# A three-way split GEMM decoder layer: the third weight tile's matmuls moved into the opening phase, five clears moved to GpSimd, and two orders changed further on

## What is computed

```python
h = rms_norm(x, norm1)
z = h @ w_in                        # 2048 x 5120: u (1024), q, f, i, g (1024 each)
pool_out = pool_mix(u)              # means over windows 2/4/8/16, a small map per group
o, S_new = hgrn2_recurrence(silu(q), 1 - forget, i, log(forget), S)   # 8 heads, state 128 x 128
o = rms(o) * hg_norm * silu(g)
x = x + concat(pool_out, o) @ w_o   # 2048 x 2048
h2 = rms_norm(x, norm2)
x = x + (silu(h2 @ w_gate) * (h2 @ w_up)) @ w_down                    # 2048 x 5632, twice, and back
return rms_norm(x, norm_f), pool state, recurrent state
```

## Time and profile before

| | |
|---|---|
| median of 3 executions | 1398.15 us (1397.76 to 1398.55) |
| the profiled execution | 1397.94 us |
| its span | 1396.1 us |
| PE busy | 1380.8 us, 10128 matmuls |
| VectorE, ScalarE, GpSimd busy | 787.9, 571.9, 204.8 us |
| mean granted clock of PE | 0.997 |

### The profile page before, as it was taken

The page is one execution under the profiler, slowest core; times in us unless marked ns, Lnnn a source line. Parts: engine busy times, 40 slices in busy tenths (PEclk is TensorE's granted clock), DMA queues, the critical chain, the costliest instruction groups (busy, mean ns, idle before and its releaser), DMA issues.

```text
span 1396.1 us, 27712 instructions
## 1 busy us (share of the span) xinstructions
PE 1380.8 (99%) x10128; PEld 1368.7 (98%) x10128; DVE 787.9 (56%) x1202; ACT 571.9 (41%) x924; POOL 204.8 (15%) x320
## 2 busy tenths in 40 slices
PE   9999999999999999999999999999999999999996
PEld 8999999999999999999999999999999999999996
DVE  7978888888655544444444444444444444444444
ACT  7546665566333333333333333333333333333442
POOL 0464444444322000000000000000000000000131
PEclk9999999999999999999999999999999999999998
DMA  9446555555655555555655545565554565555453
GB/s 321 149 124 172 163 152 152 152 157 163 176 148 150 141 157 140 150 138 145 165 147 151 150 132 146 154 169 150 150 150 121 155 172 149 152 143 149 113 157 119
DMA packets 395563, 214.50 MB, mean 154 GB/s; under 512 B 4287, under 2 KB 391487, under 8 KB 394886
## 3 DMA queue, kind: packets, MB, share of 16 engines
q1 hardware_dynamic: 377063, 203.52, 52.5%
q10 hardware_dynamic: 18470, 10.59, 2.6%
HBM read 206.43 MB, written 7.89 MB: 154 GB/s over the span
## 4 chain that ended last, share of the span: by engine, by line
PE 96%; DVE 2%; issue 1%; ACT 1%; DMA 0%; SPq 0%; DVEq 0%; ACTq 0%
PE bank L405 30%; PE bank L407 30%; PE bank L406 30%; DVE w_lo L1086 1%; DMA x_res<-in_x_turned 0%; PE bank L607 0%; DVE yg L1532 0%; PE bank L653 0%; PE bank L582 0%; PE bank L655 0%; PE bank L654 0%; PE bank L445 0%; PE bank L447 0%; PE bank L446 0%; PE bank L536 0%
## 5 line engine op out<-in xcount | busy, mean ns | idle before, releaser
L405 PE MATMUL bank<-a_hi,w_hi 128*128 128x320 f32 x2016 | 626.3, 311 | 0.1
L407 PE MATMUL bank<-a_hi,w_lo 128*128 128x320 f32 x2016 | 623.8, 309 | 0.0
L406 PE MATMUL bank<-a_lo,w_hi 128*128 128x320 f32 x2016 | 623.7, 309 | 0.0
L1086 DVE TENSOR_TENSOR w_lo<-w_raw,w_hi 128x1024 fp32r<-128x1024 f32 (+1 forms) x412 | 456.5, 1148 | 134.3 <-ACT w_hi L743 133.0
L743 ACT ACTIVATE w_hi<-w_raw 128x1024 fp32r<-128x1024 f32 (+1 forms) x412 | 383.3, 967 | 159.6 <-PE bank L407 144.8
L405 PEld LDWEIGHTS bank<-a_hi,w_hi 128*128 128x128 f32 x2016 | 378.6, 188 | 2.6 <-issue 2.1
L406 PEld LDWEIGHTS bank<-a_lo,w_hi 128*128 128x128 f32 x2016 | 378.7, 188 | 0.4
L407 PEld LDWEIGHTS bank<-a_hi,w_lo 128*128 128x128 f32 x2016 | 378.6, 188 | 0.0
L405 PE MATMUL bank<-h_hi,w_hi 128*128 128x320 f32 x704 | 217.7, 309 | 0.3 <-DVE w_lo L1086 0.3
L406 PE MATMUL bank<-h_lo,w_hi 128*128 128x320 f32 x704 | 217.6, 309 | 0.0
L407 PE MATMUL bank<-h_hi,w_lo 128*128 128x320 f32 x704 | 217.6, 309 | 0.0
(11 more groups left out here) (247 smaller groups left out, 1152.2 us busy)
## 6 DMA issues: line engine op xcount, KB each, us to landing
w_raw<-in_w_gate SPq DMA_DIRECT2D x44, 1024.0 KB, 5.6
w_raw<-in_w_up SPq DMA_DIRECT2D x44, 1024.0 KB, 5.6
w_raw<-in_w_down SPq DMA_DIRECT2D x64, 704.0 KB, 4.8
w_raw<-in_w_in SPq DMA_DIRECT2D x32, 1024.0 KB, 5.8
w_raw<-in_w_o SPq DMA_DIRECT2D x16, 1024.0 KB, 6.0
w_raw<-in_w_first_pool SPq DMA_DIRECT2D x5, 1024.0 KB, 5.5
s<-in_state_hgrn ACTq DMA_DIRECT2D x8, 512.0 KB, 4.4
out<-sn ACTq DMA_DIRECT2D x8, 512.0 KB, 5.4
```

Source lines behind the costliest of these rows:

```text
L405: pe.matmul(out, whi[:, par_, cols], r_hi, start=(k == 0), stop=False)
L406: pe.matmul(out, whi[:, par_, cols], r_lo, start=False, stop=False)
L407: last = pe.matmul(out, wlo[:, par_, cols], r_hi, start=False, stop=(k == last_k))
L1086: dve.tensor_tensor(wlo[:, par_, cols], raw[:, par_, cols], whi[:, par_, cols].bitcast(F32), SUB)\
```

## The change

It has four parts.

1. The third tile gets buffers of its own (`whi_t`, `wlo_t`, `raw_t`, over space that the FFN uses later). SP issues its halves behind chunks 3 and 7, with no wait. PE runs its first half behind k = 7 of the opening and its second behind k = 15 (`third_half`), in the same bank SC. ScalarE writes `third_hi(0)` and `square(0)` between k = 7 and k = 8 and `third_hi(1)` behind k = 15, then square(4), the first half of tile 3 (behind its load), two squares, the second half. VectorE has the low pieces in the same places, and the second low piece of tile 3 behind fold 3.
2. Of the six clears one (`qm`) stays on VectorE; the other five are GpSimd's, behind `keys(0)`. ScalarE's wait and a new one of VectorE, ahead of the first `turn`, are for all five (`sc_zero` 5).
3. Output tiles: `rec_back` of the last head stands behind 7 k-tiles of tile 1 instead of 10, and tile 1 keeps three k-tiles for the end instead of one.
4. In the last down projection `split_hi(nd + 2, 0)` stands ahead of `y_part(0)` and the table load, and every later `y_part` one split further back.

The diff, cut to its core; in order it touches the buffers, SP, PE, ScalarE, VectorE and GpSimd.

```diff
+        whi_t, wlo_t, raw_t = passing([("w_hi_third", [P, KD * P], F32R), ("w_lo_third", [P, KD * P], F32R),
+                                       ("w_raw_third", [P, KD * P], F32)])
...
             for chunk in range(len(CHUNKS)):
                 first_weights(sp, chunk)
                 load_x(sp, chunk)
+                if CHUNKS[chunk][1] % 8 == 0:
+                    p = CHUNKS[chunk][1] // 8 - 1
+                    k0, k1 = HALF[p]
+                    sp.dma_start(raw_t[:, k0 * P:k1 * P].rearrange("p (k c) -> p k c", c=P),
+                                 w_first_pool[0][:, k0:k1, :]).then_inc(w2_loaded[p], 16)
...
-            sp.wait_ge(first_lo, 4)
-            for p, tiles in enumerate(HALF):
-                pool_tile(2, 0, tiles).then_inc(w2_loaded[p], 16)
             sp.wait_ge(first_lo, len(CHUNKS))
             pool_tile(3, 1).then_inc(w3_loaded, 16)
...
+            def third_half(p):
+                pe.wait_ge(hi_ready, p + 1)
+                pe.wait_ge(lo_ready, p + 1)
+                for k in range(*HALF[p]):
+                    cols = slice(k * P, (k + 1) * P)
+                    pe.matmul(SC[:, 0:N], whi_t[:, cols], a_hi[:, k, :], start=(k == 0), stop=False)
+                    pe.matmul(SC[:, 0:N], whi_t[:, cols], a_lo[:, k, :], start=False, stop=False)
+                    last = pe.matmul(SC[:, 0:N], wlo_t[:, cols], a_hi[:, k, :], start=False, stop=(k == KD - 1))
+                return last
...
+                if k == HALF[0][1] - 1:
+                    pe.wait_ge(fill_done, 3)
+                    third_half(0)
+            third_half(1).then_inc(piece_used, 2)
...
-            pe.wait_ge(fill_done, 3)
-            unit(U0 + 2, 0, a_rhs, own_bank=SC, read=0)
...
-            part_of(1, 0, 10)
+            part_of(1, 0, 7)
             rec_back(HEADS - 1)
-            part_of(1, 10, own)
+            part_of(1, 7, 13)
...
             part_of(0, own, KD, used=1)
-            part_of(1, own, KD, used=2)
+            part_of(1, 13, KD, used=2)
...
+            def third_hi(p):
+                act.wait_ge(w2_loaded[p], 16)
+                cols = slice(HALF[p][0] * P, HALF[p][1] * P)
+                act.activation(whi_t[:, cols], raw_t[:, cols], ACT.Copy).then_inc(hi_ready, 1)
...
+                if k == HALF[0][1] - 1:
+                    third_hi(0)
                 if k in BEHIND:
                     first_piece(BEHIND.index(k) + 1)
-            square(0)
-            act.wait_ge(w2_loaded[0], 16)
-            hi_piece(2, 0, 0, HALF[0])
+                if k == HALF[0][1] - 1:
+                    square(0)
+            third_hi(1)
             square(4)
-            act.wait_ge(w2_loaded[1], 16)
-            hi_piece(2, 0, 1, HALF[1])
+            act.wait_ge(w3_loaded, 16)
+            hi_piece(3, 1, 0, HALF[0])
             square(8)
             square(12)
-            act.wait_ge(w3_loaded, 16)
-            hi_piece(3, 1, 0, HALF[0])
             hi_piece(3, 1, 1, HALF[1])
...
-            act.wait_ge(sc_zero, 1)
+            act.wait_ge(sc_zero, 5)
...
                     split_hi(nd + 1, 1, HALF_D)
+                    split_hi(nd + 2, 0, HALF_D)
                     y_part(0)
                     act.activation(warm[:, 1:2], epst[:, 0:1], ACT.Sqrt)
-                    split_hi(nd + 2, 0, HALF_D)
-                    y_part(1)
                     with act.Fori(1, KD // 2 - 1) as j:
                         split_hi(nd + 2 * j + 1, 1, HALF_D)
+                        y_part(2 * j - 1)
+                        split_hi(nd + 2 * j + 2, 0, HALF_D)
                         y_part(2 * j)
-                        split_hi(nd + 2 * j + 2, 0, HALF_D)
-                        y_part(2 * j + 1)
                     split_hi(nd + KD - 1, 1, HALF_D)
+                    y_part(KD - 3)
...
+            def third_lo(p):
+                dve.wait_ge(hi_ready, p + 1)
+                cols = slice(HALF[p][0] * P, HALF[p][1] * P)
+                dve.tensor_tensor(wlo_t[:, cols], raw_t[:, cols], whi_t[:, cols].bitcast(F32), SUB).then_inc(lo_ready, 1)
...
+                if k == HALF[0][1] - 1:
+                    third_lo(0)
...
-            lo_piece(2, 0, 0, HALF[0])
+            third_lo(1)
             lower_bound_max()
...
             fold(xsq[:, 0:4, :], xsq[:, 0:4, :], xsq[:, 4:8, :], 1)
-            lo_piece(2, 0, 1, HALF[1])
+            lo_piece(3, 1, 0, HALF[0])
             dve.wait_ge(xsq_act, 4)
             fold(xsq[:, 8:12, :], xsq[:, 8:12, :], xsq[:, 12:16, :], 2)
-            lo_piece(3, 1, 0, HALF[0])
             fold(xsq[:, 0:4, :], xsq[:, 0:4, :], xsq[:, 8:12, :], 3)
             lo_piece(3, 1, 1, HALF[1])
...
-            dve.memset(sc[:, :, :], 0.0)
-            dve.memset(qm[:, :], 0.0)
-            dve.memset(vt[:, 2, :], 0.0)
-            dve.memset(k3[3 * HS:P, :, :].bitcast(F32), 0.0)
-            dve.memset(vm[3 * HS:P, :, :, :].bitcast(F32), 0.0)
-            dve.memset(scs[:, :], 0.0).then_inc(sc_zero, 1)
-            dve.wait_ge(sc_zero, 1)
+            dve.memset(qm[:, :], 0.0).then_inc(qm_clear, 1)
+            dve.wait_ge(qm_clear, 1)
             queries(0)
             values(H0 + 2, 0)
             split_lo(H0 + 4, 0)
+            dve.wait_ge(sc_zero, 5)
...
             keys(0)
+            pool.wait_ge(st_tr, NG)
+            pool.wait_ge(mp_lo_s, HEADS)
+            for n, part in enumerate((vt[:, 2, :], k3[3 * HS:P, :, :].bitcast(F32), sc[:, :, :], scs[:, :],
+                                      vm[3 * HS:P, :, :, :].bitcast(F32))):
+                pool.memset(part, 0.0).then_inc(sc_zero, 1)
+                pool.wait_ge(sc_zero, n + 1)
             rec_sample(0)
```

More of the change, by code:

```diff
@@ L213, in hybrid_kernel @@
         ahi_ready, alo_ready = (sem(n) for n in ("ahi_ready", "alo_ready"))
-        t_ones, tails_ready, sc_zero, acc_zero, pad_zero, cache_tr, cache_in, win_step, win_ready, fix_ready, pooled_ready, po_hi_s, po_lo_s = (
-            sem(n) for n in ("t_ones", "tails_ready", "sc_zero", "acc_zero", "pad_zero", "cache_tr", "cache_in", "win_step", "win_ready", "fix_ready",
+        t_ones, tails_ready, sc_zero, qm_clear, acc_zero, pad_zero, cache_tr, cache_in, win_step, win_ready, fix_ready, pooled_ready, po_hi_s, po_lo_s = (
+            sem(n) for n in ("t_ones", "tails_ready", "sc_zero", "qm_clear", "acc_zero", "pad_zero", "cache_tr", "cache_in", "win_step", "win_ready", "fix_ready",
                              "pooled_ready", "po_hi_s", "po_lo_s"))
@@ L346, in _, with pool_tile @@
                 load_x(sp, chunk)
-            def pool_tile(n, par_, tiles=(0, KD)):
-                k0, k1 = tiles
-                return sp.dma_start(raw[:, par_, k0 * P:k1 * P].rearrange("p (k c) -> p k c", c=P),
-                                    w_first_pool[n - 2][:, k0:k1, :])
+                if CHUNKS[chunk][1] % 8 == 0:
[3 more added lines that the diff above has]
+                                 w_first_pool[0][:, k0:k1, :]).then_inc(w2_loaded[p], 16)
+            def pool_tile(n, par_):
+                return sp.dma_start(raw[:, par_, :].rearrange("p (k c) -> p k c", c=P), w_first_pool[n - 2])
             sp.dma_start(cst[:, C_ID:C_ID + P], consts[:, C_ID:C_ID + P]).then_inc(ident_loaded, 16)
-            sp.wait_ge(first_lo, 4)
-            for p, tiles in enumerate(HALF):
-                pool_tile(2, 0, tiles).then_inc(w2_loaded[p], 16)
             sp.wait_ge(first_lo, len(CHUNKS))
```

## The result

The changed kernel takes 1400.13 us (median of 22 runs, 1398.35 to 1401.59), the kernel before 1398.22 (22 runs, 1397.48 to 1399.60): ratio 1.0015, interval 1.0009 to 1.0020. That is 1.9 us slower. It lies inside the 0.2% and inside the range's outer edge (1400.2), but the forecast was no move, and its sign is clear.

A forecast was written before the change was run, and what follows sets the result against it. PE was taken to bound the kernel, with at most 1.95 us of its idle time to win. Opening +1.33, clears -0.4, output tiles -0.4, last splits -0.45 sum to +0.08: median 1398.2 us, range 1396.4 to 1400.2.

The forecast's parts named there:

- the landing of the fourth tile: Opening: load of tile 3 of slot 1, issued at 19.95, takes 5.5 us and lands at 25.2, as PE frees the slot.
- The chain behind the landing: Opening: high piece, two squares, second high piece, folds and second low piece follow the landing; PE may go on at 33.0.
- the load rival: Opening: fourth tile's load takes 9 us, lands at 29, costs 3.6 more; +3.7 in all, 1401.8; chance 0.06.
- The delay of ScalarE in the opening: Opening: two extra ScalarE operations, 1.05 and 1.26, plus a 0.3 load wait make it some 2.4 us later.
- The first gap: Opening, near 14.0: PE stalls 0.45 for the third tile's first half; bounds 0 and 1.3.
- The gap of 0.95 in the fourth tile: Opening, near 32: PE waits 0.95 for that tile's second low piece; bounds 0 and 2.
- The 0.1 for the norm's sum: End of the opening: folds 4 and 5 end at 34.15, so PE starts the norm's sum 0.1 later.
- Part 2: Clears moved to GpSimd: gain 0.4 of the 0.86 lost at the first `rec_out`; bounds 0.5 lost to 0.86 gained.
- the general lock: Part 2: if clears blocked behind eight `queries` instructions they would end past 101, a loss near 1; not charged.
- Parts 3 and 4: Output tiles: gain 0.4 of 0.46, bounds -0.3 and 0.46; last down projection's splits: gain 0.45, bounds 0 and 0.46.
- The opening is free: Rival: the opening's order costs nothing and all four waits go, -1.95, 1396.2; chance 0.17.
- The opening costs more and GpSimd is late: Rival: opening +2.3 (fourth tile a microsecond late), clears gain 0, other parts -0.85; +1.5, 1399.7; chance 0.17.

The follow-up runs named there:

- e10_early_halves: Changed kernel with the fourth tile loaded in halves, behind the sixth and the eighth first low piece: 1399.11 us, ratio 1.0006 against the kernel before.
- e16_late_again: Changed kernel with cache, masks and the loads behind them held until the fourth tile's first high piece, profiled a second time: 1401.56 us, one run.
- e9_cache_late: Changed kernel with cache, masks and the two loads behind them issued only after the fourth tile's first high piece: 1402.14 us, ratio 1.0030 against before.
- e1_opening: Kernel before with part 1 alone (third tile inside the opening): 1402.57 us, ratio 1.0033.
- e15_cache_early: Changed kernel with the cache and mask loads issued ahead of the fourth tile's wait and load: 1400.72 us, ratio 1.0018 against the kernel before.
- e14_again: The changed kernel itself, unaltered, in the second of two repeat profiles: 1401.18 us.
- e13_again: The changed kernel itself, unaltered, in the first of two repeat profiles: 1400.33 us.
- e6_load_alone: Changed kernel with unit 4's tile and the pooling weights loaded only after the fourth tile's first high piece: 1400.45 us, ratio 1.0014 against before.
- e12_best: Kernel before with parts 2 to 4, without part 1, and ScalarE's split moved ahead of its wait for the clears: 1396.14 us, ratio 0.9984.
- e3_tiles: Kernel before with part 3 alone (output tiles): 1397.52 us, ratio 0.9994.
- e4_splits: Kernel before with part 4 alone (ScalarE's order in the last down projection): 1397.23 us, ratio 0.9995.
- e8_all_three: Changed kernel with squares and folds first, unit 4's tile and pooling weights held back, third tile's first half two k-tiles later on PE: 1399.33 us, ratio 1.0011.
- e2_clears: Kernel before with part 2 alone (five clears on GpSimd): 1398.16 us, ratio 1.0000.

## Why the prediction was wrong

**The step that failed is the landing of the fourth tile**, "there is nothing ahead of it in the queue a little sooner. I take 25.2 for both". The issue time was right to 0.2, and so was the release of the slot, counted from PE: ScalarE went on 10.9 us behind the third tile's first matmul in `e10_early_halves` (14.95, 25.86) and `e16_late_again` (14.52, 25.42), 10.75 predicted. The load took 7.5, not the 5.5 of the earlier trace rows. I took one duration from one row as a property of the tile, while the same 1 MB took 5.1 to 7.5 in the profiles of this study. The cache and masks behind it were in my text and costed only as late themselves, not as engine time. What the runs showed in its place: with those two loads held back the tile took 5.8 and 5.2 us in this opening; with them close behind it, 6.4 to 7.5 in six profiles and 5.1 in one. Why it varies so stays open.

**The chain behind the landing was right to a tenth.** Predicted: landing 25.2, `rms_first` and the next unit 1.33 late, at 33.23 + 1.33 = 34.56, so 9.36 behind the high piece. Measured in the profiles with this order, start of the high piece and of the unit behind the norm's sum:

| kernel | high piece | unit | difference |
|---|---|---|---|
| `e16_late_again` | 25.42 | 34.90 | 9.48 |
| `e10_early_halves` | 25.86 | 35.33 | 9.47 |
| `e9_cache_late` | 26.03 | 35.50 | 9.47 |
| `e1_opening` | 26.63 | 36.09 | 9.46 |
| `e15_cache_early` | 27.51 | 36.98 | 9.47 |
| `e14_again` | 27.58 | 37.05 | 9.47 |
| `e13_again` | 27.59 | 37.05 | 9.46 |
| after | 27.68 | 37.15 | 9.47 |
| `e6_load_alone` | 28.14 | 37.60 | 9.46 |

Each microsecond of landing is one of PE's, as the load rival said. The high piece 2.48 later than 25.2 and the tenth in the chain are the 2.59 between the shift of 3.92 and the 1.33 forecast. Not all of the 2.48 is the load's: where it is in time, the slot's release sets the high piece at 25.86 (`e10_early_halves`) or 25.42, so 0.2 to 0.7 would have been missed anyway. That rival priced 9 us and +3.7; at 7.5 us its own rule gives 27.6 - 25.3 = 2.3 more than the forecast, 1400.5, against 1400.13. Its mechanism was right, and 0.06 was too little for it. The argument against it, that the loads ahead are gone by then, was true and beside the point, since the loads that took its share stood behind.

**The smaller terms of the opening.** The delay of ScalarE in the opening was added up wrong: 1.05, 1.26 and 0.3 are 2.6, not 2.4, and 17.53 + 2.6 is the 20.1 at which the load was issued. The first gap was 0.80, not 0.45: the half tile landed so that its high piece began at 12.15 instead of 11.95, and PE was done 0.2 sooner. It cost nothing in the end, since the chain hangs on the landing: `e14_again`, whose PE lost over a microsecond at k = 2, was at the norm's sum with the others. The gap of 0.95 in the fourth tile is 1.70 in the kernel after and 1.06 in `e10_early_halves`. The two large gaps share one length from the landing; which of them it falls into depends on when PE arrives. The 0.1 for the norm's sum can't be seen apart.

**Part 2** gained 0.38 in the whole change (predicted 0.4), and 0.40 alone. That the number fits is in part luck: the sum took all of it from the wait for `s1`, whose gap fell only from 0.85 to 0.66; the other half came from the late start at 102.87 that the sum did not have. The fifth clear, against the 99.5 predicted plus the shift of 3.9; timeline of GpSimd after:
```profile
99.73 0.55 POOL L1613 TENSOR_TENSOR km<-kp,ones_mat 128x128 f32<-128x128 f32 x1
100.42 0.61 POOL L1621 TENSOR_TENSOR kp<-kp,t 128x64 f32<-128x64 f32 x2
...
102.23 0.95 POOL L1638 MEMSET vm<- 32x1024 f32 x1
```
It ends at 103.18, where 99.5 + 3.9 is 103.4. The clear of 1024 elements took 0.95, as its size gives (0.09 + 0.87), with VectorE at work beside it all the time. The five `queries` operations beside the five clears took 0.47 each, against 0.45 in the kernel before. So a clear neither blocks nor is blocked there, as the Trainium skill, SBUF — State Buffer, section Who interferes with whom, has it for an instruction that only writes. No run shows the general lock, which I had weighed against this part, on a clear. What I did not see is that the cheap cure stood beside it: ScalarE's split needs no clear at all, and with the clears on GpSimd it can go ahead of the wait for them (`e12_best`).

**Parts 3 and 4** gained 0.52 and 0.50 (predicted 0.4 and 0.45), and each wait is gone in the kernel that has its part alone.

**The other rivals.** "The opening is free" fell: even with the load in time it costs some 2 us (`e10_early_halves`, 2.1 against one profile of before). "The opening costs more and GpSimd is late" came nearest by number (1399.7), and its first half, a landing a microsecond late, was the right direction; its second was wrong. Against the sum: +1.33 was +3.92, -1.25 was -1.40, and the tail added 0.6 in the profiled execution.

## What to carry to other kernels

A load's duration in a trace belongs to the traffic around it: before moving one, add up the engine time, not the bytes, of all that is in flight, behind it as well as ahead. A buffer that fills an engine's spare time also takes the slack that hid the next hand-over; look for the chain that begins at the old buffer's release, since everything in it then counts in full (here 9.47 us from the high piece to the next unit, in nine profiles). And where a wait guards several instructions, ask first which of them needs it: moving one split out from behind it, with the three small parts, beat every version of the large one.

## What the runs showed of the hardware

- **Bytes are not DMA time.** The engines were full at 222 to 269 GB/s with the cache and masks, and moved 403 with weight tiles. The same 1024 KB, issued near 20, took 5.2 and 5.8 us alone, 6.4 to 7.5 with the two right behind in six profiles and 5.1 in one, and 5.3 to 6.4 in six profiles of the old opening.
- **The last matmul pair** took 0.81 us in the kernel before and in `e3_tiles`, `e4_splits`, `e8_all_three` and `e13_again`, 1.07 in `e2_clears`, and 1.33 to 1.44 in the other twelve profiles; for the kernel after the clock in the windows around it (columns as in the windows above) is:
```profile
1386.50:1388.50 2.00, 0.23 (x2) 0.18 (x2) 1.22 (x6) 0.42 (x2) 0.00 (x0) 0.94 0.00 0
1388.50:1390.50 2.00, 1.26 (x2) 0.32 (x2) 0.64 (x1) 0.00 (x0) 0.00 (x0) 0.50 0.00 0
```
The granted clock is 0.94 and then 0.50, the lower of its two levels (1.2 GHz), after PE had been busy 0.23 of 2 us. That is 0.6 us on a path where nothing hides it, and it differs between executions of one kernel (`e13_again` 0.81, `e14_again` 1.43). Shorter windows show why: in the kernel after the granted clock fell at about 1388.25, just ahead of the pair at 1388.32; in `e2_clears` it fell within the pair; in `e13_again` it fell at about 1389.1, when the pair, begun at 1388.25, was through.
- **GpSimd beside VectorE's splits.** Part 4 brought the squares of the last down projection beside splits with two SBUF inputs: they took 1.56 us in the mean, where they took 0.72 before. It cost nothing, since nobody waits for it.
